# Sixteen units of an FFN in seven block products each, instead of eight

## What is computed

```python
h = rmsnorm(x, norm_ffn[l])
gt, up = jnp.split(h @ w_ffn_in[l], 2, axis=-1)          # 1024 -> 2 x 2816
x = x + ((jax.nn.silu(gt) * up) @ w_ffn_out[l]).astype(x.dtype)
return rmsnorm(x, norm_final)
```

## Time and profile before

| what | value |
|---|---|
| median of 3 executions | 794.04 us (792.46 to 794.29) |
| profiled execution, its own time | 792.53 us |
| span of the profiled execution | 790.7 us |
| TensorE busy | 782.2 us, 99% |
| VectorE, ScalarE, GpSimd busy | 457.6, 309.4, 105.3 us |
| first FFN matrix, first to last unit | about 429.5 to 664.5 us |
| mean granted TensorE clock | 0.998 of full |

### The profile page before, as it was taken

One profiled execution on the slowest core, in us unless ns is written; L12 is line 12 of the kernel. 1 busy time (PEld: TensorE's weight loads), 2 busy tenths in 40 slices (PEclk: granted clock), 3 DMA queues, 4 the chain that ended last, 5 costly groups with the idle time before them and its releaser, 6 DMA issues.

```text
span 790.7 us, 11974 instructions
## 1 busy us (share of the span) xinstructions
PE 782.2 (99%) x4670; PEld 666.1 (84%) x4670; DVE 457.6 (58%) x895; ACT 309.4 (39%) x552; POOL 105.3 (13%) x75
## 2 busy tenths in 40 slices
PE   9999999999999999999999999999999999999996
PEld 7878899889878787788888888999999998888885
DVE  5935432645766876657527698666666655422347
ACT  6212155243646566642316352333323323222235
POOL 1301000000000000002200671433333300000000
PEclk9999999999999999999999999999999999999999
DMA  7931345340311111145331533333333334222202
GB/s 236 346 121 54 107 93 148 73 122 4 108 54 54 54 54 42 41 146 145 134 109 75 139 106 107 107 106 106 106 106 105 93 127 155 106 107 106 106 1 106
DMA packets 101274, 83.32 MB, mean 105 GB/s; under 512 B 16960, under 2 KB 94832, under 8 KB 101232
## 3 DMA queue, kind: packets, MB, share of 16 engines
q1 hardware_dynamic: 100992, 82.46, 34.9%
q10 hardware_dynamic: 240, 0.29, 0.1%
HBM read 77.44 MB, written 5.29 MB: 105 GB/s over the span
## 4 chain that ended last, share of the span: by engine, by line
PE 98%; DMA 0%; ACT 0%; issue 0%; DVE 0%; ACTq 0%; DVEq 0%
PE bank L1699 28%; PE bank L1700 28%; PE bank L1701 28%; PE bank L1932 2%; PE bank L1951 2%; PE bank L1919 2%; PE bank L1833 1%; PE bank L1874 1%; PE bank L1855 1%; PE bank L1796 1%; PE bank L1740 1%; PE bank L1946 1%; PE bank L1746 0%; PE bank L1749 0%; PE bank L1723 0%; PE bank L1886 0%
## 5 line engine op out<-in xcount | busy, mean ns | idle before, releaser
L1023 DVE TENSOR_TENSOR w_lo<-w_raw,w_hi 128x2048 fp32r<-128x2048 f32 (+2 forms) x29 | 64.5, 2225 | 79.8 <-ACT w_hi L660 79.8
L1699 PE MATMUL bank<-n_hi,w_hi 128*128 128x512 f32 x272 | 108.8, 400 | 0.0
L1701 PE MATMUL bank<-n_hi,w_lo 128*128 128x512 f32 x272 | 106.1, 390 | 0.0
L1700 PE MATMUL bank<-n_lo,w_hi 128*128 128x512 f32 x272 | 106.0, 390 | 0.0
L1699 PE MATMUL bank<-h_hi,w_hi 128*128 128x512 f32 (+1 forms) x272 | 99.5, 366 | 0.8 <-issue 0.8
L1700 PE MATMUL bank<-h_lo,w_hi 128*128 128x512 f32 (+1 forms) x272 | 99.1, 364 | 0.0
L1701 PE MATMUL bank<-h_hi,w_lo 128*128 128x512 f32 (+1 forms) x272 | 99.0, 364 | 0.0
L660 ACT CAST w_hi<-w_raw 128x2048 fp32r<-128x2048 f32 (+2 forms) x29 | 53.6, 1848 | 61.8 <-PE bank L1701 51.0
L1699 PE MATMUL bank<-w_hi,a_hi 128*128 128x512 f32 (+1 forms) x180 | 69.2, 385 | 0.0
L1700 PE MATMUL bank<-w_lo,a_hi 128*128 128x512 f32 (+1 forms) x180 | 69.2, 384 | 0.0
L1701 PE MATMUL bank<-w_hi,a_lo 128*128 128x512 f32 (+1 forms) x180 | 69.2, 384 | 0.0
(11 more groups left out here) (287 smaller groups left out, 1598.8 us busy)
## 6 DMA issues: line engine op xcount, KB each, us to landing
w_raw<-in_w_ffn_in_dram SPq DMA_DIRECT2D x44, 512.0 KB, 5.1
w_raw<-in_w_in_dram SPq DMA_DIRECT2D x37, 512.0 KB, 4.8
w_raw<-in_w_ffn_out_dram SPq DMA_DIRECT2D x22, 512.0 KB, 3.7
w_raw<-in_w_out_dram SPq DMA_DIRECT2D x8, 512.0 KB, 3.7
w_raw<-in_w_in_dram SPq DMA_DIRECT2D x12, 256.0 KB, 4.5
xs<-in_x_dram SPq DMA_DIRECT2D x4, 512.0 KB, 4.9
wck_k<-in_w_ck_dram SPq DMA_DIRECT2D x1, 2048.0 KB, 11.9
wck_v<-in_w_cv_dram SPq DMA_DIRECT2D x1, 2048.0 KB, 13.6
```

Source lines behind the costliest of these rows:

```text
L1023: dve.tensor_tensor(wlo[u % 2][:, 0:n], raw[u % 2][:, 0:n], whi[u % 2][:, 0:n].bitcast(F32), ALU.subtract).then_inc(lo_done, 1)
L1699: pe.matmul(dst, w[0], x_[0], start=start, stop=False)
L1700: pe.matmul(dst, w[0], x_[1], start=False, stop=False)
L1701: return pe.matmul(dst, w[1], x_[0], start=False, stop=stop)
```

## The change

- Units 6 to 21 are all seven units (16 instead of 8); units 1 to 5 and 22 stay plain. Both weight slots now hold sums and parts, so each slot has its own places for the plain parts (`ahi7`, `alo7`). The sums s7 lie in the low slot of the unit (`wlo`), and `sums_lo` writes over them in place.
- The loops are gone: each engine's queue is written out unit by unit.
- TensorE's order in a seven unit: M1, plain block with a sum of h, plain block with plain h (into M1's bank, after M1's copy), then the three products of sums, then the sum with plain h. Even and odd units use banks 0 to 3 and 4 to 7.
- VectorE writes four of its seven additions back to PSUM; ScalarE writes tanh to PSUM. The gate scale and the last multiplication read two banks in one instruction (`twin`).
- GpSimd starts t after the low parts of unit 3, and makes a unit's sums as the products of the unit two before it free the blocks of the low slot.
- The down projection starts with tiles 0 and 1 instead of 2 and 3.

```diff
-SEVEN_FROM = 5
-SEVEN_N = (FT - 1 - SEVEN_FROM) // 2
+SEVEN = tuple(range(5, 21))
+        s7 = [at(f"weight_sums{j}", [4, 4, P], B + 4 * SLOT * (4 + j)) for j in range(2)]
...
             pool.wait_ge(h_lo, 2 * TT)
-            pool.wait_ge(r_ready, 2)
+            pool.wait_ge(lo_done, U_IN + 3)
...
+            for u in SEVEN:
+                k, s = sevens(u), u % 2
+                w = slot_view(raw, s, KC, 256)
+                pool.wait_ge(raw_full[s], raw_count(U_IN + u))
+                if u - 2 in SEVEN:
+                    pool.wait_ge(m_done, 7 * sevens(u - 2) + 5)
+                else:
+                    pool.wait_ge(*multiplied(u - 2))
+                pool.tensor_tensor(s7[s][:, 2], w[:, 0:4, 0:P], w[:, 0:4, P:256], ALU.subtract).then_inc(s_sums, 1)
+                if u - 2 in SEVEN:
+                    pool.wait_ge(m_done, 7 * sevens(u - 2) + 6)
+                pool.tensor_tensor(s7[s][:, 0], w[:, 0:4, P:256], w[:, 4:8, P:256], ALU.add).then_inc(s_sums, 1)
+                pool.wait_ge(s_sums, 4 * k + 2)
+                pool.tensor_tensor(s7[s][:, 1], s7[s][:, 0], w[:, 0:4, 0:P], ALU.subtract).then_inc(s_sums, 1)
+                pool.wait_ge(*multiplied(u - 2))
+                pool.wait_ge(s_sums, 4 * k + 3)
+                pool.tensor_tensor(s7[s][:, 3], w[:, 4:8, 0:P], s7[s][:, 1], ALU.subtract).then_inc(s_sums, 1)
...
+            for u in range(4, FT):
+                if u + 1 in SEVEN:
+                    plain_hi(u + 1)
+                tanh_gate(u - 1)
+                if u in SEVEN:
+                    keep_m1(u)
+                if u + 1 in SEVEN:
+                    sums_hi(u + 1)
+                else:
+                    unit_hi(u + 1)
...
+            def early_sums(u):
+
+                k, a = sevens(u), 4 * (u % 2)
+                dve.wait_ge(m1_out, k + 1)
+                dve.wait_ge(m_done, 7 * k + 3)
+                dve.tensor_tensor(ps[a][:, 256:512], ps[a][:, 256:512], m1s[:], ALU.add).then_inc(u_sums, 1)
+                dve.wait_ge(m_done, 7 * k + 4)
+                dve.tensor_tensor(u2s[:], ps[a + 1][:, 0:256], m1s[:], ALU.add).then_inc(u_sums, 1)
+
+            def late_sums(u):
+
+                k, a = sevens(u), 4 * (u % 2)
+                dve.wait_ge(u_sums, 7 * k + 2)
+                dve.wait_ge(m_done, 7 * k + 5)
+                dve.tensor_tensor(u3s[:], ps[a + 2][:, 0:256], u2s[:], ALU.add).then_inc(u_sums, 1)
+                dve.wait_ge(u_sums, 7 * k + 3)
+                dve.wait_ge(m_done, 7 * k + 6)
+                dve.tensor_tensor(ps[a + 3][:, 256:512], ps[a + 3][:, 0:256], u3s[:], ALU.add).then_inc(u_sums, 1)
+                dve.tensor_tensor(u4s[:], ps[a + 3][:, 0:256], u2s[:], ALU.add).then_inc(u_sums, 1)
+                dve.tensor_tensor(ps[a + 2][:, 256:512], ps[a + 2][:, 256:512], u3s[:], ALU.add).then_inc(u_sums, 1)
...
+            for u in range(4, FT):
+                scaled_gate(u - 1)
+                if u + 1 in SEVEN:
+                    plain_lo(u + 1)
+                gated(u - 1)
+                if u in SEVEN:
+                    early_sums(u)
+                if u + 1 in SEVEN:
+                    sums_lo(u + 1)
+                else:
+                    unit_lo(u + 1)
+                if u in SEVEN:
+                    late_sums(u)
...
+                pe.wait_ge(wa_lo, 2 * k + 2)
+                pe.wait_ge(gu_free, u + 1)
+                product(a, 0, plain(0, 4), turned(0, early))
+                pe.wait_ge(t_lo, 4)
+                product(a + 2, 256, [v[s][1][:] for v in (ahi7, alo7)], mixed(3))
+                pe.wait_ge(m1_out, k + 1)
+                product(a, 256, plain(4, 8), turned(4, early))
+                pe.wait_ge(hi_done, U_IN + u + 1)
+                pe.wait_ge(lo_done, U_IN + u + 1)
+                product(a + 1, 0, summed(1), mixed(1))
+                product(a + 2, 0, summed(2), mixed(2))
+                product(a + 3, 0, summed(0), mixed(0))
+                pe.wait_ge(u_sums, 7 * k + 2)
+                product(a + 1, 256, summed(3), turned(4, late))
```

More of the change, by code:

```diff
@@ L81, with sevens, plains @@
 HALVES_NSA = (4, 2)
+def sevens(u):
+    return sum(v < u for v in SEVEN)
+def plains(u):
+    return u - sevens(u)
 def schedule():
@@ L320, in trunk @@
         x2_kept = nc.dram_tensor("x2_kept", (S, D), F32, kind="Internal").ap()
-        ps = [ctx.enter_context(nc.psum_tensor(f"bank{i}", [P, 512], F32)) for i in range(8)]
+        twin = [ctx.enter_context(nc.psum_tensor(f"bank{i}", [P, 2, 512], F32)) for i in range(4)]
+        ps = [twin[i // 2][:, i % 2, :] for i in range(8)]
         x_in = [sem(f"x_in{q}") for q in range(4)]
@@ L627, in _ @@
-            pool.tensor_tensor(t_f[:, 2], t_f[:, 2], l_f[:, first, late], ALU.subtract).then_inc(t_made, 1)
+            link(pool.tensor_tensor(t7[:, 2], h_f[:, second, late], h_f[:, first, late], ALU.subtract))
+            link(pool.tensor_tensor(t7[:, 2], t7[:, 2], l_f[:, second, late], ALU.add))
+            pool.tensor_tensor(t7[:, 2], t7[:, 2], l_f[:, first, late], ALU.subtract).then_inc(t_made, 1)
             pool.wait_ge(t_made, 1)
-            link(pool.tensor_tensor(t_f[:, 1], t_f[:, 2], h_f[:, first, early], ALU.add))
@@ L630, in _ @@
[L630 removed]
+            link(pool.tensor_tensor(t7[:, 1], t7[:, 2], h_f[:, first, early], ALU.add))
+            pool.tensor_tensor(t7[:, 1], t7[:, 1], l_f[:, first, early], ALU.add).then_inc(t_made, 1)
             pool.wait_ge(t_made, 2)
[L632 to L633 removed]
@@ L635, in weight_sums @@
[L635 to L646, removed]
@@ L648, in _ @@
-            weight_sums(0, True)
-            with pool.Fori(1, SEVEN_N) as i:
-                weight_sums(i)
+            link(pool.tensor_tensor(t7[:, 3], h_f[:, second, early], t7[:, 1], ALU.subtract))
+            pool.tensor_tensor(t7[:, 3], t7[:, 3], l_f[:, second, early], ALU.add).then_inc(t_made, 1)
+            for u in SEVEN:
[15 more added lines that the diff above has]
+                pool.tensor_tensor(s7[s][:, 3], w[:, 4:8, 0:P], s7[s][:, 1], ALU.subtract).then_inc(s_sums, 1)
@@ new lines, in plain_hi, with sums_hi @@
+            def plain_hi(u):
+                s = u % 2
+                act.wait_ge(raw_full[s], raw_count(U_IN + u))
+                same = [v for v in SEVEN if v < u and v % 2 == s]
+                if same:
+                    act.wait_ge(m_done, 7 * sevens(same[-1]) + 3)
+                w = slot_view(raw, s, KC, 256)
+                act.copy(ahi7[s][0][:], w[:, :, 0:P]).then_inc(wa_hi, 1)
+                act.copy(ahi7[s][1][:], w[:, 4:8, P:256]).then_inc(wa_hi, 1)
+            def sums_hi(u):
+                s = u % 2
+                act.wait_ge(*multiplied(u - 2))
+                act.wait_ge(s_sums, 4 * sevens(u) + 4)
+                act.copy(shi7[s], s7[s][:]).then_inc(hi_done, 1)
@@ new lines, in keep_m1, with tanh_gate, part_of_t @@
+            def keep_m1(u):
+                k = sevens(u)
+                act.wait_ge(m_done, 7 * k + 1)
+                if k:
+                    act.wait_ge(u_sums, 7 * k - 5)
+                act.copy(m1s[:], ps[4 * (u % 2)][:, 0:256]).then_inc(m1_out, 1)
+            def tanh_gate(u):
+                s = u % 2
+                act.wait_ge(g_scaled, u + 1)
+                act.activation(ps[4 * s][:], gs[:, s, :], ACT.Tanh, scale=0.5).then_inc(gu_tanh, 1)
+            def part_of_t(n, b):
+                if b:
+                    act.wait_ge(t_made, n + 1)
+                else:
+                    act.wait_ge(t1_made, 3)
+                act.copy(thi[:, b], t7[:, b]).then_inc(t_hi, 1)
```

361 lines of the change are left out of this document (113 added, 248 removed).

## The result

The kernel with the change takes 797.19 us (median of 5 executions, 797.11 to 799.03); the kernel before took 794.03 us beside it (5 executions, 792.46 to 794.29). The ratio is 1.0052, 95% interval 1.0036 to 1.0068: slower by 0.5%, 3.2 us, where 797.2 us had been predicted. The profiled execution took 797.48 us (span 795.7).

What follows compares the result with a forecast made beforehand. TensorE, busy 99% of the span, was taken as the bound; -7.8 - 0.9 + 8.0 + 3.9 = +3.2 us gave a median of 797.2 us, range 791.0 to 800.0 us.

Steps and rivals of the forecast that it cites:

- eight units, plain to seven: Units 7, 9, ... 21 turned from plain to seven products: 0.97 us of TensorE saved each, -7.8 us.
- even slots' plain blocks at another pace: Even slots' plain-block products, at new places, might run at 120 ns instead of 114: +1.2 us, kept for the range.
- stall before unit 3: TensorE's 1.17 us wait at 453, while VectorE's low parts run beside GpSimd's sums of h, would go: -0.9 us.
- from unit 8 on: In 14 units, TensorE waits for m1 while VectorE and GpSimd block each other: 0.57 us each, +8.0 us (0 to +11.3).
- beginning: Late t and two units' sums in a row delay m1: +0.8 in unit 6, +3.1 in unit 7, together +3.9 us.
- alternation of a late and a free unit: From unit 8 on: strict alternation gives 10.7 us per unit; with an occasional second free unit, 10.5 us was taken.
- ring: TensorE's product 3 waits for m1, queued behind tanh, gate scale, block sums and low parts: 9.25 us alone, under 9.93.
- reader: Shared thing that keeps two-SBUF-input VectorE operations and GpSimd operations from running together; wanted 9.38 of 9.93 us per seven unit.
- The rival of the full cover: GpSimd and VectorE interleave without blocking, as their busy sum just allows: 785.3 to 789.2 us, chance 0.14.
- where TensorE wanted to go on at 499.6: Unit 7: m1 ready at 502.6, TensorE wanting to continue at 499.6, so +3.1 us with the restart.
- Priced at nothing: Weight loads, the reload of x2, ScalarE's work, unrolling and block sums written to PSUM (0.42 us taken): 0 us.
- The signs to look for: Gaps of 0.4 to 1.6 us ahead of product 3 in about every second unit; about 3 us in unit 7.

Runs made afterwards that it cites:

- Run 4: Changed kernel with VectorE's plain low parts of the next unit moved behind the two steps finishing the unit before: 788.83 us (single).
- run 1: Changed kernel with the copy m1 put ahead of the previous unit's tanh in ScalarE's queue: 788.45 us, ratio 0.9931 to the kernel before.
- run 2: Changed kernel with GpSimd's four weight sums per unit replaced by memsets, so that GpSimd writes but reads nothing there: 784.58 us (single).
- run 3: Changed kernel with VectorE's four late block sums placed ahead of the low parts of the next unit: 813.28 us (single).
- run 8: Kernel before, with GpSimd's sums of h started only after unit 3's low parts are made: 804.05 us (single), 9.7 us slower than before.
- run 7: On run 1, only the region with the odd slot's plain high parts and both slots' plain low parts moved 64 bytes lower: 788.06 us (single).
- run 9: On the kernel with both queue reorderings (786.64 us), weight slots put an odd multiple of 64 bytes from inputs, h and t: 790.85 us.
- run 10: On the kernel with both queue reorderings (786.64 us), only tiles ahead of the weight slots moved by 64 bytes against the weights: 790.92 us (single).
- run 6: On run 1, every SBUF tile moved 64 bytes lower: 789.13 us (single), every pace as before.

## Why the prediction was right

**The total.** Forecast of the span: +3.2 us; measured +5.0 by the two profiled executions (790.7 to 795.7), +3.2 by the medians (794.03 to 797.19). The profiled execution before lay 1.5 us under the median and that after 0.3 us over it, so part of the hit is luck of 1.8 us. The terms can be checked one by one, by starts:

| term | forecast | measured |
|---|---|---|
| eight units, plain to seven | -7.8 us | -7.9 (8 x (10.91 - 9.92), a unit without a stop) |
| even slots' plain blocks at another pace | 0, range to +1.2 | +0.9 (24 matmuls x 4.5 ns in eight units) |
| stall before unit 3 | -0.9 | -0.9 |
| from unit 8 on | +8.0 (0.57 per unit) | +8.2 (see below) |
| beginning | +3.9 | +4.3, restarts included |
| outside the FFN's first matrix | 0 | +0.4 |

They add up to +5.0, as the span does.

- **TensorE's work** was right where a row had the price. The even slots' pace was known to be open; I took 114 and it is 117.8.
- **From unit 8 on:** unit 8 starts at 510.46 and unit 22 at 658.50, 148.04 / 14 = 10.57 us per unit; forecast 10.5. Over 9.93 that is 0.64 a unit, 9.0 us, of which 0.8 is the pace above in seven units: 8.2 for the stops, 0.59 a unit. (Run 4, without a stop, takes 139.6 us from unit 8 to unit 22: 8.4 less.) The working behind the 0.57 was an alternation of a late and a free unit, joined by a second free one now and then. The trace has the fixed pattern of none, short and long instead; that the mean came out the same is in part luck. The mechanism (ring and reader) is the one that was named: run 1 cuts the ring at m1 and the stops ahead of product 3 go, run 2 takes the reader from GpSimd and all go, run 3 lengthens the ring and every unit stops.
- **The rival of the full cover** (785.3 to 789.2) is what the kernel does with two queue orders changed: 786.64. So its reasoning, that all work fits by the sums, was sound; what spoke against it, the queues in order, is what stood in the way. I had called that a matter of the reader's load (9.38 of 9.93 us). Run 4 has the same load and no steady stop: the order made the blocking fall on the ring. That a load close to full is what lets the order matter is argued, no run lowers it alone.
- **The beginning** was right in sum and wrong in its split: unit 6's stop ahead of product 3 was put at 0.8 and is 1.9, unit 7's at 3.1 and is 1.7, and 0.87 ahead of product 1 of unit 6 hadn't been seen (there VectorE's plain low parts and the steps that free banks stand behind the low parts of t, which end at 482.5). The step that failed is "where TensorE wanted to go on at 499.6": the two earlier stops bring it to product 3 of unit 7 at 501.6, and m1, copied from 502.8 where the working had the end of the copy at 502.6, is late from then only. Errors of both signs shared one sum, since a delay once taken isn't taken again.
- **Priced at nothing, rightly:** loads, the reload of x2, the unrolling. The block sums written to PSUM take 0.41 to 0.43 us, the tanh 0.60 where it took 0.63. The Trainium skill ("ScalarE: Activation LUTs", Step-by-step) has ScalarE's writes to PSUM faster than those to SBUF; the trace agrees, with 0.03 us here.
- **The signs to look for** held: stops ahead of product 3, m1 behind tanh behind the gate scale, low parts of 3.1 to 3.3 us. From unit 8 on 9 of the 14 units have a stop, four of them a long one, where about every second had been named. Two signs didn't hold: the 3 us in unit 7, and the stop ahead of product 1, which I had named as a sign of the wrong queue and which occurs once.
- **A slip beside the sum:** by the prediction's own terms the time equals the old one at 10.27 us per seven unit (4.8 us over 14 units, above 9.93), not at 10.2. The forecast doesn't use it.
- Not shown: what the stall's 0.9 us is worth by itself (run 8 shows its cause, and loses more elsewhere), and what GpSimd's speed and GpSimd's reads each are worth (run 2 changes both). Neither was tried further.

## What to carry to other kernels

When a change doubles the work beside TensorE, the busy shares tell whether it fits, and the queues in order tell whether it will: follow each copy that frees a bank back through its queue, and put it ahead of anything that waits for another engine. Here two such moves, of no instruction more or less, turned 0.5% slower into 1% faster. Put VectorE's operations with two SBUF inputs where GpSimd has nothing to read; where both must run, look at the distribution of durations (minimum, median, maximum), since a mean hides a lock.

## What the runs showed of the hardware that was not expected

- The distance of the stationary from the moving tile changes TensorE's pace at the full clock: 256-column matmuls start 113 to 120 ns apart on average, 512-column ones 227 to 233.3, by shifts of 64 bytes (runs 7, 9, 10); a shift of all tiles together changed nothing (run 6). In runs 9 and 10 an odd multiple of 64 bytes was better for 256 columns and worse for 512. The rule behind it stays open. A layout changed for another reason can move a kernel by 4 us this way.
- After a pause of 7.6 us the granted clock was 0.51 for 5.7 us, and matmuls of 512 columns started 0.43 us apart (run 8). No shorter stop had this effect: the windows around those of the kernel after (up to 1.9 us) show 1.00, and so do those around the 2.3 us of run 3.
